# Neighbourhood attention on one core: where a finished tile is copied, which units carry output blocks, and where a spread stands

## What is computed

```
s_loc = q_r . k_r + bias, masked to 16 columns around the query     (8 rows of keys)
s_ctx = q_r . k_context
p     = softmax(concat(s_loc, s_ctx))
y_n   = p_loc @ v_r + p_ctx @ v_context
yc_n  = softmax(qc . kc) @ vc            only where need_ctx (layer 0)
out   = concat(y_m, y_n) @ w_out         then gate, residual, norm, MLP
```

## Time and profile before

| what | value |
| --- | --- |
| median of 3 runs | 3403.2 us (3399.94 to 3404.34) |
| profiled execution, its own time | 3403.29 us |
| its span in the profile | 3401.5 us |
| mean granted clock of TensorE | 0.99 |
| TensorE busy | 3332.3 us, 98% |
| VectorE (DVE) busy | 1626.1 us, 48% |
| ScalarE (ACT) busy | 1220.5 us, 36% |
| GpSimd (POOL) busy | 1797.0 us, 53% |

### The profile page before, as it was taken

The page is one execution under the profiler, slowest core; times in us unless marked ns, Lnnn a source line. Parts: engine busy times, 40 slices in busy tenths (PEclk is TensorE's granted clock), DMA queues, the critical chain, the costliest instruction groups (busy, mean ns, idle before and its releaser), DMA issues.

```text
span 3401.5 us, 49617 instructions
## 1 busy us (share of the span) xinstructions
PE 3332.3 (98%) x17286; PEld 2748.5 (81%) x17286; DVE 1626.1 (48%) x2523; ACT 1220.5 (36%) x1977; POOL 1797.0 (53%) x2004
## 2 busy tenths in 40 slices
PE   8999999999999999999999999999999999999998
PEld 6778888888768888888888778888888788778887
DVE  4533257788643238778746445211212754442113
ACT  4433343233434233333434553321212434533222
POOL 5325568887434558888365223433334464246555
PEclk9999999999999999999899999999999999999999
DMA  4212345454312335554243112212212442133323
GB/s 171 83 48 93 99 139 183 167 173 140 109 59 68 94 98 186 175 179 172 100 128 91 51 48 96 63 62 63 65 61 66 123 116 75 62 108 108 99 93 105
DMA packets 105271, 358.48 MB, mean 105 GB/s; under 512 B 11872, under 2 KB 20320, under 8 KB 103200
## 3 DMA queue, kind: packets, MB, share of 16 engines
q1 hardware_dynamic: 70560, 257.13, 23.4%
q10 hardware_dynamic: 34560, 99.30, 9.0%
HBM read 336.79 MB, written 8.59 MB: 102 GB/s over the span
## 4 chain that ended last, share of the span: by engine, by line
PE 66%; POOL 15%; issue 13%; DVE 3%; ACT 2%; DMA 1%; ACTq 0%; POOLq 0%; DVEq 0%; SPq 0%
POOL w_lo L576 15%; PE ps L1019 9%; PE ps L1020 9%; PE ps L1021 9%; PE ps L670 4%; PE ps L672 4%; PE ps L671 4%; PE ps L1127 3%; PE ps L1128 3%; PE ps L1129 3%; PE ps L925 2%; PE ps L927 2%; PE ps L926 2%; PE ps L1438 1%; PE ps L1278 1%
## 5 line engine op out<-in xcount | busy, mean ns | idle before, releaser
L576 POOL TENSOR_TENSOR w_lo<-w_raw,w_hi 128x256 fp32r<-128x256 f32 x1904 | 1690.7, 920 | 1554.6 <-ACT w_hi L1486 1541.3
L1486 ACT ACTIVATE w_hi<-w_raw 128x1024 fp32r<-128x1024 f32 x472 | 498.9, 1057 | 752.8 <-PE ps L1021 336.1
L670 PE MATMUL ps<-h_hi,w_hi 128*128 128x512 f32 x944 | 373.1, 395 | 0.0
L671 PE MATMUL ps<-h_lo,w_hi 128*128 128x512 f32 x944 | 368.5, 390 | 0.0
L672 PE MATMUL ps<-h_hi,w_lo 128*128 128x512 f32 x944 | 368.4, 390 | 0.0
L2329 DVE SCALAR_TENSOR_TENSOR ada_junk<-ada_w,c_silu 128x1024 f32<-128x1024 f32 x192 | 318.6, 1659 | 3.3
L1127 PE MATMUL ps<-c_hi,w_hi 128*128 128x512 f32 (+1 forms) x832 | 300.2, 361 | 6.5 <-DVE c_lo L2518 3.7
L1128 PE MATMUL ps<-c_lo,w_hi 128*128 128x512 f32 (+1 forms) x832 | 287.9, 346 | 0.0
L1129 PE MATMUL ps<-c_hi,w_lo 128*128 128x512 f32 (+1 forms) x832 | 287.5, 346 | 0.0
L1019 PE MATMUL ps<-c_hi,w_hi 128*128 128x512 f32 (+1 forms) x768 | 274.0, 357 | 2.5 <-DVE c_lo L2518 2.5
L1020 PE MATMUL ps<-c_lo,w_hi 128*128 128x512 f32 (+1 forms) x768 | 274.0, 357 | 0.0
(11 more groups left out here) (380 smaller groups left out, 6095.3 us busy)
## 6 DMA issues: line engine op xcount, KB each, us to landing
w_raw<-in_w SPq DMA_DIRECT2D x476, 512.0 KB, 3.5
ada_w<-in_ada ACTq DMA_DIRECT2D x96, 512.0 KB, 3.6
zs<-stage ACTq DMA_DIRECT2D x52, 128.0 KB, 2.1
m_row<-m_spill ACTq DMA_DIRECT2D x16, 384.0 KB, 5.4
wq_row<-wq_spill ACTq DMA_DIRECT2D x16, 384.0 KB, 5.6
x_spill<-x ACTq DMA_DIRECT2D x2, 2048.0 KB, 6.7
zs_m<-zm ACTq DMA_DIRECT2D x32, 128.0 KB, 2.6
bias<-in_rpb ACTq DMA_DIRECT2D x8, 512.0 KB, 4.1
```

Of the source, the lines that this page charges most:

```text
L576: last = nc.gpsimd.tensor_tensor(w_lo[:, j, c], w_raw[:, j % RAW, c], w_hi[:, j, c].bitcast(F), ALU.subtract)
L670: nc.tensor.matmul(bank, w_hi[:, j, w], rhs_hi[:, k, :], start=(k == 0), stop=False)
L671: nc.tensor.matmul(bank, w_hi[:, j, w], rhs_lo[:, k, :], start=False, stop=False)
L1486: nc.scalar.activation(w_hi[:, j, :], w_raw[:, j % RAW, :], ACT.Copy).then_inc(hi_ready, 1)
```

## The change

Three edits. On ScalarE, in layer 0 (`need_ctx`) alone, the takes of a unit stand ahead of its exponentials and not behind them. On TensorE the early output blocks are shared out over all units of `rest`, the first included: in layer 0 shares of 3, 4, 3, 4, 3, 4 for units 18 to 23 in place of 0, 4, 4, 4, 4, 5; in layer 1 shares of 3, 3, 3, 3 for units 12 to 15 in place of 0, 4, 4, 4. And the spread of layer 0 (the wait for `diag_f` and the matmul at L1327) stands behind the seven context blocks of output tile 1.

```diff
@@ TensorE, neighborhood
                 for i, u in enumerate(rest):
                     if u + 1 < len(units):
                         scores(u + 1)
-                    if i:
-                        share = early[(i - 1) * len(early) // (len(rest) - 1):i * len(early) // (len(rest) - 1)]
-                        for c, k, part in share:
-                            if k == 0 and part == X:
-                                out_arrive(c)
-                            if k == 0:
-                                taken(("nk" if (c, part) == (0, X) else "nv", 3))
-                            last = out_block(c, k, part)
-                            if (c, k, part) == early[0]:
-                                last.then_inc(chunk_used, 3)
+                    for c, k, part in early[i * len(early) // len(rest):(i + 1) * len(early) // len(rest)]:
+                        if k == 0 and part == X:
+                            out_arrive(c)
+                        if k == 0:
+                            taken(("nk" if (c, part) == (0, X) else "nv", 3))
+                        last = out_block(c, k, part)
+                        if (c, k, part) == early[0]:
+                            last.then_inc(chunk_used, 3)
                     weighted(u - 1)
                     by_key(u)
...
                 pe.wait_ge(npt_copied, base + len(units))
+                for k in range(KT - 1):
+                    for part in both:
+                        if (1, k, part) not in early:
+                            out_block(1, k, part)
                 if L == 0:
                     pe.wait_ge(nlo_ready, H2)
                     pe.wait_ge(both_v, 4)
                     nc.tensor.matmul(ps[:, 7, :], ones, diag_f[:, :, :].rearrange("p t q -> p (t q)"), start=True, stop=True).then_inc(rb_f_ready, 1)
-                for k in range(KT - 1):
-                    for part in both:
-                        if (1, k, part) not in early:
-                            out_block(1, k, part)
@@ ScalarE, attention
                     if u >= 1:
                         by_key(u - 1)
+                    if need_ctx:
+                        for p in tiles_after(u, units, need_ctx, 0, 0):
+                            take(p)
                     act.wait_ge(nneg_ready, base + (u + 1))
...
                     last.then_inc(nexp_done, 1)
-                    for p in tiles_after(u, units, need_ctx, 0, 0):
-                        take(p)
+                    if not need_ctx:
+                        for p in tiles_after(u, units, need_ctx, 0, 0):
+                            take(p)
```

## The result

The changed kernel takes 3409.9 us (median of 11 runs, 3407.8 to 3413.5) against 3402.7 us before (11 runs beside them): the ratio is 1.0022, 95% interval 1.0015 to 1.0030. It is slower by 7.2 us: little, but the interval is clear of no change. The forecast was 3407.6 us in a range of 3401.5 to 3411. The profiled execution takes 3409.1 us, its span is 3407.3.

The account below looks back on a forecast made before the run. TensorE, busy 98% of the span, was taken to bound the kernel. From the profiled 3403.3 us, -3.66 - 1.59 + 4.1 - 1.63 + 4.1 + 1.4 + 1.6 = +4.3 gave 3407.6 us, range 3401.5 to 3411.

Parts of the forecast that it names:

- The zn waits and the clock behind the first: Layer 0: both 1.83 us TensorE waits for zn go (-3.66), and one half-clock loss (-1.59).
- the fourth rival: Layer 0's even units: exponentials pushed 2.23 us later reach TensorE, up to 13 us, 3421 us; chance 0.04.
- Layer 0's first last unit: At the first output block TensorE waits 4.1 us for w_lo in place of 2.5; +1.5 us in all.
- Layer 0's second last unit: Context blocks need DVE's copy of tile 28 into vn; TensorE waits 2.7 us, +2.6 net.
- The clock in layer 0: Behind the first last unit's longer wait, the half-clock loss was left as it was before.
- the second rival: Late weight costs more: a second clock fall at layer 0's vn wait, another in layer 1; 3410.8 us; chance 0.20.
- The spread: Layer 0: seven context blocks cover TensorE's 1.63 us wait for diag_f, -1.63 us.
- Layer 1: Layer 1's last units: a longer wait for w_lo, less cover and a clock fall, +7.1 us together.
- The wait: Layer 1's first output block: TensorE waits 4.72 us for w_lo in place of 0.64, +4.1 us.
- The cover: Layer 1's last two units: three blocks a unit in place of four cover less, 0.7 us each, +1.4.
- slower by more than can be told: Whole kernel: a time above 3410.0 us, beyond the 6.8 us a measurement can tell from no change; chance 0.22.
- One cost was priced at nothing: ScalarE, layer 0: exponentials start up to 2.23 us later at six even units, hidden by cover; priced at 0.

Follow-up runs that it names:

- e4: The kernel before with layer 1's shares 3, 3, 3, 3 and nothing else; 3408.2 us, ratio 1.0025.
- e8: The changed kernel with layer 0's takes put back behind the exponentials; 3418.8 us, ratio 1.0051.
- e5: e2 with the upper-half matmuls of layer 0's first four output blocks at unit 18, their lower-half matmuls still at unit 19; 3399.0 us.
- e7: The changed kernel with six grid blocks ahead of layer 0's context blocks, in shares of 3, 3, 4, 4, 3, 4; 3408.2 us.
- e3: The changed kernel except that layer 1 keeps its old shares of 0, 4, 4, 4; 3400.5 us, ratio 0.9999.
- e1: The kernel before with only layer 0's takes moved ahead of the exponentials; 3398.5 us, ratio 0.9992.
- e2: e1 plus the spread moved behind the seven context blocks, output blocks shared out as before; 3397.4 us, ratio 0.9986.
- e11: The changed kernel with each layer's first-last-unit output blocks behind the weighting and ahead of by_key; 3406.5 us, ratio 1.0014.
- e9: The kernel before with the spread moved and, in layer 0, only value tiles' copies into zn ahead of the exponentials, every split behind; 3393.7 us, ratio 0.9977.

## Why the prediction was right

It went by terms, so it is checked by terms, in the profiled executions. The mechanism was right: the blocks come ahead of a weight half that is late in both layers, and cost more than the takes and the spread win. The size came out low by 1.5 us in the spans and 2.9 in the medians.

- **The zn waits and the clock behind the first** (-3.66 and -1.59): both waits are gone, and from the `zn` transposes to the weighting it is 4.76 us at both places (1934.32 - 1929.56, 1977.33 - 1972.57), against 6.44 and 4.85. Right, as far as the two executions go. The 1.59 us were partly luck: of the six `zn` waits in the traces of the kernel before, e4 and e8, two were followed by a fall of the clock. No wait for probabilities came at the six even units; the fourth rival is out.
- **Layer 0's first last unit** (4.1 us for `w_lo` in place of 2.5): 4.09 us. Right.
- **Layer 0's second last unit** (2.7 us for `vn`): 2.46 us. Right. e5 and e7 add what the step did not say: the wait is `weighted(18)`'s own as well, so taking the context blocks away leaves 0.85 us of it.
- **The clock in layer 0** was mis-sized. The step left its loss as before, 1.6 us. It fell twice: the grid blocks lost 4.07 - 2.2 = 1.9 us, and behind the wait for `vn` three context blocks took 2032.00 - 2029.78 = 2.2 us, where e3 at full clock took 1.4, and the weighting 0.5 more: 1.3. (In e3 the clock fell as well, 0.9 us later, and took 1.4 us from the weighting and the transposes.) So 3.2 us in place of 1.6. This is the half of the second rival that came true. Stage 0 grew by 6.4 us in place of the 4.1 of the sum, and these 1.6 are most of the difference; 0.7 us is spread over the stage and stays untraced.
- **The spread** (-1.63): the first blocks of output tile 0 behind it come at 2058.85 against 2058.65 (second matmul), while `weighted(23)` is 1.9 us late: -1.7. Right; the seven blocks covered it, and the spread's later place held nothing up.
- **Layer 1** (+7.1): 6.9 us, and 6.7 in e4 alone. The wait, 4.63 against 0.64 us (+4.0, forecast +4.1). The clock, three blocks from 2971.72 to 2975.57 = 3.9 in place of 2.2 (+1.7, forecast +1.6). The cover (+1.4) had about the right size in another place than named: 0.7 us at the weighting of unit 12, which waits for tile 28's values and grew from 0.62 to 1.33, and 0.5 at the `by_key` waits together; the copy of unit 15 still waits 1.17 us. `by_key` of unit 12 comes 8.3 us after its old place in the layer (7 forecast, without the clock).

The sum forecast +4.3; the spans differ by 5.8 and the medians by 7.2. Stretch by stretch the spans differ by +1.2 us up to a `scores` early in layer 0's attention (1888.03 against 1886.83), -5.7 from there to `scores(19)`, +6.4 in stage 0, -2.1 to layer 1's last units, +6.9 in stage 1 and -0.9 behind it. The first and the last are no part of the edit as far as the traces show, and nearly cancel. The middle four stand against -5.25, +4.1, -1.63 and +7.1 of the sum, so the miss lies mostly in stage 0, and there in the second fall of the clock.

The median of 3409.9 us lies 1.1 us inside the end of the range, and 0.1 us under the 3410.0 us beyond which the prediction would have called it slower by more than can be told. That it fell on this side is luck.

One cost was priced at nothing and is none in the changed kernel, only because a larger wait hides it: the split ahead of the exponentials, which delays them by 0.5 us at a value tile (they start 2.01 us behind `scores(19)` in place of 1.50) and makes GpSimd run beside DVE's scalings, another 0.8. In e1 and e2, where no block stands in unit 18, it shows as 3.8 us at `by_key` in place of 2.5. In the changed kernel `by_key` starts at 2023.62, over 4 us after the scalings are done. The prediction had named the delay of ScalarE and not the one of DVE.

Much of the scatter between runs of one kernel goes with the clock. Of the 89 runs of the kernel before beside the experiments, the 18 with a mean granted clock of 0.989 took 3405.5 us on average, and the 25 with 0.991 took 3399.9. Averaged over its runs the clock is 0.9902 before and 0.9886 in the changed kernel, which is some 10 us more at 1.2 GHz in each execution (an estimate: twice the difference, times the span). The traces of the two profiled executions show 69 and 79 us of it. What stays open is at which waits it falls in the runs that have no profile.

## What to carry to other kernels

A wait of an engine is filled only by work whose own inputs are there by then: look up when the last of them lands (here the lower half of a weight, at the end of a chain over ScalarE and GpSimd) before moving a block into the gap, and put it behind the work that others wait for, not ahead. In every timeline here TensorE's matmuls keep the order of the program, so a block ahead of the chain that paces the stage cost its wait in full, and a little more at the waits behind it (e11: 0.45 and 0.67 us). When a copy is moved forward, move only the part that someone waits for; what hangs on its end (here a split that starts GpSimd) can stay behind.

## What the runs showed of the hardware

DVE's scaling of 128 x 512 by a column (TENSOR_SCALAR, SBUF to SBUF) has a longest of 962 ns in the changed kernel and of 489 ns before; the medians, 485 and 481 ns (80 scalings, 16 of them half as wide), hide it. All of the long ones, two at each of the six takes whose unit has scalings this wide, lie beside GpSimd's subtractions of two SBUF tiles, 0.70 us each, and none is long in e9, where the two hardly overlap:

```profile
L2629 DVE TENSOR_SCALAR sn<-sn,tiny x80: 346/485/962, 1890.0 to 2993.7; 128x512 f32<-128x512 f32 x64, 128x256 f32<-128x256 f32 x16
```

```profile
L2633 DVE TENSOR_SCALAR sn<-sn,tiny x80: 345/481/489, 1892.0 to 2981.2; 128x512 f32<-128x512 f32 x64, 128x256 f32<-128x256 f32 x16
```

GpSimd pays as well: its four take 2.96 us beside the scalings and 2.80 alone. The Trainium skill ("SBUF — State Buffer", Who interferes with whom) says that DVE's tensor_scalar can enter a mode that uses a port pair shared with GpSimd, and that the one that comes second is blocked for the other's whole instruction. The trace agrees. Each scaling ends 0.28 us after a subtraction does, wherever it began, and the subtraction between them takes 0.90 us in place of 0.72:

```profile
2017.33 0.72 POOL L576 TENSOR_TENSOR w_lo<-w_raw,w_hi 128x256 fp32r<-128x256 f32 x1
2017.51 0.82 DVE L2629 TENSOR_SCALAR sn<-sn,tiny 128x512 f32<-128x512 f32 x1
...
2018.01 0.90 POOL L576 TENSOR_TENSOR w_lo<-w_raw,w_hi 128x256 fp32r<-128x256 f32 x1
2018.25 0.94 DVE L2629 TENSOR_SCALAR sn<-sn,tiny 128x512 f32<-128x512 f32 x1
```

TensorE's clock fell to its 1.2 GHz level behind some waits and not behind others of the same length. Of the waits in the attention of the two layers, in all 14 traces, three of the ten of 1.6 to 1.9 us were followed by a fall, seven of the nine of 2.0 to 2.5 us, and twelve of the thirteen of 3.5 us and more (the one without is the 3.50 us of e11). A fall cost the matmuls behind it 1.3 us (the change, at 2029.7) to 2.8 us (e2, at `by_key` of unit 18).
